# Layer 0 of a streaming encoder step in three parts: the 32-row sample alone first, the second prompt tile's input projection behind the sample's queries

## What is computed

```python
def peer(h, w_query, sub_keys, u_emb, v_emb):
    ...
        qry = (xb @ w_query).astype(f32).reshape(PEER_BLOCK, PEER_HEADS, 2, PEER_DQ // 2)
        sc = jnp.einsum('thpd,pnd->thpn', qry, sub_keys.astype(f32))
        s1, i1 = lax.top_k(sc[:, :, 0], PEER_TOPK)
        s2, i2 = lax.top_k(sc[:, :, 1], PEER_TOPK)
    ...
        top_s, sel = lax.top_k(cand_s, PEER_TOPK)
        idx = jnp.take_along_axis(cand_i, sel, axis=-1)
        gate = jax.nn.softmax(top_s, axis=-1)
        act = jax.nn.gelu(jnp.einsum('thed,td->the', u_emb[idx], xb).astype(f32))
        return jnp.einsum('the,thed->td', (gate * act).astype(xb.dtype), v_emb[idx])

def trunk(x, st_a_conv, st_a_delta, st_b_conv, st_b_h, c_k, c_v, p, past):
    ...
    for l in range(DEPTH):
        h = rmsnorm(x, p['norm_mix'][l])
        ...
        x = x + out
        x = x + peer(rmsnorm(x, p['norm_ffn'][l]), p['peer_w_query'][l], p['peer_sub_keys'][l],
                     p['peer_u'][l], p['peer_v'][l])
```

## Time and profile before

| | us |
|---|---|
| median of 3 runs (lowest, highest) | 1945.54 (1941.55, 1947.11) |
| the profiled execution | 1943.43 |
| its span | 1941.7 |
| PE busy | 1212.1 |
| DVE busy | 1225.5 |
| ACT busy | 723.0 |
| POOL busy | 726.5 |
| TensorE clock granted, mean of the span | 0.738 |

### The profile page before, as it was taken

The page is one execution under the profiler, slowest core; times in us unless marked ns, Lnnn a source line. Parts: engine busy times, 40 slices in busy tenths (PEclk is TensorE's granted clock), DMA queues, the critical chain, the costliest instruction groups (busy, mean ns, idle before and its releaser), DMA issues.

```text
span 1941.7 us, 25073 instructions
## 1 busy us (share of the span) xinstructions
PE 1212.1 (62%) x9288; PEld 739.9 (38%) x9288; DVE 1225.5 (63%) x3079; ACT 723.0 (37%) x1937; POOL 726.5 (37%) x651
## 2 busy tenths in 40 slices
PE   7998865566667539855579546665666644444443
PEld 7896742233335307733248224443325400000000
DVE  4541558888755575476654674557865667677664
ACT  2322145534432335274333333237533334333322
POOL 2021024545433433333133444434533444454442
PEclk9999875676788859966689658778679955555555
DMA  5645389999999999999599999999999999999996
GB/s 192 205 142 162 126 319 397 421 388 421 420 418 418 419 421 393 417 418 393 205 373 416 420 421 417 418 419 414 375 420 418 420 421 422 422 420 422 421 421 273
DMA packets 115658, 720.74 MB, mean 371 GB/s; under 512 B 13424, under 2 KB 13552, under 8 KB 41296
## 3 DMA queue, kind: packets, MB, share of 16 engines
q0 software_dynamic: 82944, 604.02, 75.6%
q1 hardware_dynamic: 31584, 113.84, 15.9%
q10 hardware_dynamic: 1008, 1.29, 0.2%
HBM read 714.98 MB, written 4.12 MB: 370 GB/s over the span
## 4 chain that ended last, share of the span: by engine, by line
DMA 46%; PE 27%; DVE 15%; ACT 6%; issue 4%; POOL 2%; ACTq 0%; POOLq 0%; DVEq 0%; SPq 0%
DMA sb_AR<-in_uv,sb_idx 44%; PE PS L1429 10%; DVE sb_AR L1011 7%; PE PS L1674 5%; PE PS L1651 2%; PE PS L1571 2%; PE PS L1694 1%; POOL sb_AR L513 1%; DMA sb_W<-in_w 1%; ACT sb_DG L576 1%; DVE sb_AR L1063 1%; ACT sb_gl L573 1%; PE PS L1815 1%; ACT L573 1%; DMA sb_lq<-in_lq 1%
## 5 line engine op out<-in xcount | busy, mean ns | idle before, releaser
L513 POOL DMA_INDIRECT sb_AR<-in_uv,sb_idx x576 | 695.2, 1207 | 1042.1 <-PE PS L1674 910.4
L1011 DVE CUSTOM_DVE_ANT_0 sb_AR<-sb_AR 128x1024 f32<-128x1024 f32 x576 | 703.9, 1222 | 452.3 <-DMA sb_AR<-in_uv,sb_idx 447.6
L1674 PE MATMUL PS<-sb_AR,sb_DG 128*32 128x256 f32 x4608 | 509.7, 528 | 582.2 <-ACT sb_DG L576 559.6
L1674 PEld LDWEIGHTS PS<-sb_AR,sb_DG 128*32 128x32 f32 x4608 | 128.9, 129 | 893.7 <-ACT sb_DG L576 802.1
L573 ACT ACTIVATE sb_gl<-sb_dots 128x1 f32<-128x1 f32 x576 | 116.2, 202 | 875.5 <-DVE sb_dots L1011 874.2
L1429 PE MATMUL PS<-sb_hT,sb_W 128*128 128x160 f32 (+1 forms) x2304 | 345.8, 310 | 8.6 <-ACT sb_hT L547 3.3
L1429 PEld LDWEIGHTS PS<-sb_hT,sb_W 128*128 128x128 f32 x2304 | 322.8, 208 | 50.6 <-issue 24.8
L576 ACT ACTIVATE sb_DG<-sb_GR,sb_gl 128x32 f32<-128x32 f32 x576 | 185.1, 321 | 18.7
L573 ACT ACT_TABLE_LOAD x68 | 87.2, 1283 | 1.1
L558 ACT ACTIVATE sb_AR<-sb_Hn 32x1024 f32<-32x1024 f32 x72 | 75.8, 1053 | 1.5
L1651 PE MATMUL PS<-sb_W,sb_mixT 128*128 128x512 f32 x128 | 69.8, 672 | 6.0 <-DMA sb_W<-in_w 4.8
(11 more groups left out here) (357 smaller groups left out, 1193.3 us busy)
## 6 DMA issues: line engine op xcount, KB each, us to landing
sb_W<-in_w SPq DMA_DIRECT2D x192, 512.0 KB, 7.9
sb_AR<-in_uv,sb_idx POOLq DMA_INDIRECT x576, 16.6
sb_gB<-in_gains SPq DMA_DIRECT2D x7, 512.0 KB, 7.7
sb_mixT<-in_kc SPq DMA_DIRECT2D x2, 1024.0 KB, 8.9
sb_hT<-in_vc SPq DMA_DIRECT2D x2, 1024.0 KB, 18.5
out_o_k<-sb_AR SPq DMA_DIRECT2D x1, 1152.0 KB, 9.2
sb_X<-in_x SPq DMA_DIRECT2D x2, 512.0 KB, 7.5
out_o_v<-sb_AR SPq DMA_DIRECT2D x1, 1024.0 KB, 14.3
```

Source lines behind the costliest of these rows:

```text
L513: g.indirect_dma_start(UV[:, sl, :], None, T[f"uv{layer}"], bass.IndirectOffsetOnAxis(ap=idx[:, c:c + 1], axis=0)).then_inc(S(f"uv_in{sl}" ...
L1011: v.tensor_tensor_reduce(UV[:, sl, 0:D], UV[:, sl, 0:D], Hrep[:, u % 2, :], 1.0, 0.0, ALU.mult, ALU.add, dots[:, sl:sl + 1]).then_inc(S("d ...
L1674: r = mm(PS[32 * q:32 * q + 32, 6 + u % 2, 0:256], DG[:, sl, :], UV[:, sl, o:o + 256], start=(c == 0), stop=(c == 31), skip_group_check=True)
```

## The change

Layer 0 is now done in three passes, `TILES = ((2,), (0,), (1,), (2, 0), (1,))`. The first 16 input blocks still run at 160 columns for the sample and tile 0; the other 8 (for `z` and the RG-LRU's gate) stand behind them as `fill` 0 to 7. Then the sample's chunk work goes alone, with 6 stages of inverse instead of 10 (its chunk is 32 long); its output blocks and its queries at 32 columns; `pick(0)`; the first gathers. Tile 0's chunk work stands between the sample's pieces; its output blocks and queries stand beside steps 1 to 24. Tile 1's 24 input blocks are `fill` 8 to 31, behind the sample's queries and beside those steps; its convolutions stand beside steps 21 to 36 and the rest of its mixer beside steps 38 to 141. Output and query weights of layer 0 are loaded once more, so there are 216 block loads.

The order on each engine is now written by `weave`, which merges generators by the keys of `PLAN`. The first 8 gathers use 4 slots only, as the other 4 still hold tile 0's mixer.

```diff
-TILES = ((0, 2), (1,), (2, 0), (1,))
...
+TILES = ((2,), (0,), (1,), (2, 0), (1,))
...
+def slot(m):
+    return m % 4 if m < M4 else (m - M4 + 4) % UVS
+
+
+def slot_before(m):
+
+    return (m - 4 if m >= 4 else None) if m < M4 else (None if m < M4 + 4 else m - UVS)
...
+INV = ["a2", "n2", "n4", "n8", "x1", "m1", "x2", "m2", "x3", "m3"]
+INVS = (INV[0:6], INV, INV)
...
+USES = [((0, "in", j), IN_F[j]) for j in range(16)] + [((2, "fill", n), IN_F[FILL[n][1]]) for n in range(32)]
+for _mp in range(5):
+    if _mp > 2:
+        USES += [((_mp, "qkv", j), B_QKV1 + j) for j in range(24)]
+    USES += [((_mp, "out", j), (B_OUT0, B_OUT1)[_mp > 2] + j) for j in range(8)]
+    USES += [((_mp, "q", j), (B_Q0, B_Q1)[_mp > 2] + j) for j in range(16)]
+USES.sort(key=lambda u: PLAN[u[0]])
+STREAM = [b for _, b in USES]
...
+def weave(*streams):
+
+    heads = [[next(g), k, g] for k, g in enumerate(streams)]
+    while heads:
+        h = min(heads, key=lambda x: x[0:2])
+        t = next(h[2], None)
...
+                    if m == M4:
+                        eng.wait_ge(S("mix_d"), 2)
+                    if b is not None:
+                        eng.wait_ge(S("vsum"), b + 1)
```

```diff
-            caches(0)
-            eng.wait_ge(S("s_qks"), 1)
-            eng.wait_ge(S("pvs"), 1)
-            caches(1)
...
+            eng.wait_ge(S("blk"), POS[2, "out", 7] + 1)
+            cache_k(0)
...
+            cache_v(0)
+            eng.wait_ge(S("s_qks"), 1)
+            cache_k(1)
+            eng.wait_ge(S("pvs"), 1)
+            cache_v(1)
```

More of the change, by code:

```diff
@@ L55, in unit_of @@
     return (2, 0) if k == 0 else ((k - 1) // 4, (k - 1) % 4)
[L58 to L81, removed]
@@ L227, in build @@
         CSi, CSo = a(16, 3), a(16, 6)
+        class VJ:
+            pass
+        class VS:
+            pass
         class V0:
@@ L311, in inv_count, with inv_ps @@
[L311 to L328 removed]
+        def inv_ps(p, name, i):
+            return (i, 0) if p else INV_S[name[0]][i]
@@ L879, in mixer1 @@
                                          ACT.Copy, scale=la_[:, 50:51]).then_inc(S("mix1"), 1)
-                for j in range(8):
-                    upto("out", j)
-                norm(FFN_NORM[mp])
-                upto("norm3")
-                evac_hT(FFN_NORM[mp])
-                queries(mp, upto)
-            mixer1(2)
-            mixer1(3)
-            run.upto(32 * 14 + 8)
-            norm(8)
-            run.upto(NSTEP)
-            norm(9)
+                yield from tail(mp)
+            weave(part0(), gates(0), part1(), fill(), early_hrep(), early_gates(), convs2(), rest(), gates(2), steps())
+            norm(11)
         @block.vector
@@ L907, in rsqrt, with norm @@
                 ch.link(v.tensor_tensor(r, r, w, ALU.mult))
-            def norm(k, last=False, between=lambda: None):
-                tiles = NORMS[k][1]
-                for i, t in enumerate(tiles):
+            def norm(k):
+                for i, t in enumerate(NORMS[k][1]):
                     R = slice(0, ROWS[t])
@@ L1280, in residual, with tail @@
+            def tail(mp):
+                yield at(mp, "norm3")
+                eng.wait_ge(S("blk"), POS[mp, "out", 7] + 1)
                 for t in TILES[mp]:
@@ L1391, in mixer1 @@
                 r.then_inc(S("os_n"), 1)
-                residual(mp, upto)
-                norm(FFN_NORM[mp], between=lambda: upto("norm3"))
-                for j in range(16):
-                    upto("q", j)
-            mixer1(2)
-            mixer1(3)
-            run.upto(32 * 14 + 8)
-            norm(8, last=True)
-            run.upto(NSTEP)
+                yield from tail(mp)
+            weave(part0(), part1(), lru0(), rest(), lru1(), early_picks(), steps())
             peer_add(NUNIT - 1)
-            norm(9, last=True)
+            norm(11)
         @block.tensor
@@ L1828, in mixer1 @@
                     r.then_inc(S("o_tr"), 1)
-                eng.wait_ge(S("mix1"), (4, 6)[ps])
-                out_proj(mp, upto)
-                upto("norm3")
-                transposes(FFN_NORM[mp])
-                hT_ready(FFN_NORM[mp])
-                queries(mp, upto)
-            mixer1(2)
-            mixer1(3)
-            run.upto(NSTEP)
+                yield from tail(mp)
+            weave(part0(), gates(0), part1(), fill(), rest(), steps())
+            assert used[0] == len(STREAM)
 def layout(inputs):
```

1766 lines of the change are left out of this document (913 added, 853 removed), and 6 rows, old and new, of tables (PLAN, _us).

## The result

The changed kernel takes 1975.72 us (median of 4 runs, 1972.66 to 1976.88), the kernel before 1945.18 (4 runs, 1941.55 to 1947.11). The ratio is 1.0161, with a 95% interval of 1.0145 to 1.0177: it is slower by 31 us. The forecast was 1926 with a range up to 1954, so it was wrong in sign and in range. The profiled execution took 1972.66 us, the fastest of the four.

What follows compares the result with a forecast made beforehand. Full DMA engines (419 to 421 GB/s) were taken to bound the long stretches with gathers, so an earlier start should pay. 1943.4 - 16 (gather 32 earlier) + 8 (tile 1's mixer) - 9 (caches) gave 1926 us, range 1891 to 1954.

Steps and rivals of the forecast that it cites:

- Bytes: Whole kernel: 24 more block loads of 0.524 MB, 12.6 MB or 30 us at 421 GB/s.
- cache mechanism: Layer 1: keys of the second half no longer wait for values of the first, removing the wait for caches.
- point of comparison: Gather 32, issued at 341.56 before: all extra blocks used by then, the same work left in both kernels.
- The path to the sample's outputs: Layer 0, ahead of the sample's queries: mixer, inverse, output blocks and norm done by 141 us.
- Nine blocks at 2.1, the first two at up to 3.6: Sample's 32-column query blocks ahead of the first gather: 26 us with tile 0's chunk work between, ending at 167.
- First dot at 192: Behind the first gather, forecast at about 174: five query blocks and the copies, then the first dot product at 192.
- sum 0 at 203: Step 0's sum on PE at 203, behind two input and two output blocks, one waiting for tile 0's mixture.
- 5.1 a step: From sum 0 to sum 24: 5.1 us a step, putting gather 32 at 325, a gain of 16.
- The three limits: Per step from sum 0 to sum 24: PE work 4.7 us, DMA transfers 4.6, landing of blocks 5.1.
- loss 8: Tile 1's convolutions beside steps 21 to 36 load DVE; landed slots absorb 24 us; loss 8, bounds 0 and 20.
- gain 9: Sample's attention in layer 1: no wait for the caches, gain 9 us, bounds 0 and 20.
- Slower: Rival: sums behind slow blocks, 6.2 us or more a step, gather 32 at 352 or later, 1956 us; chance 0.17.

Runs made afterwards that it cites:

- Experiment 2: The changed kernel with 33 useless matmuls filling PE's pauses between the sample's output blocks and its queries, still 32 columns wide; 1973.82 us, ratio 1.0159.
- experiment 1: The changed kernel with the sample's 16 query blocks run over 128 columns instead of 32, the extra results unread; 1956.98 us, ratio 1.0073 to the kernel before.
- Experiments 5: experiment 1 with the four copies of the sample's rows put behind query blocks 2 to 5 on ACT, not behind the last; 1954.27 us, ratio 1.0062.
- experiment 6: Experiments 5's kernel with tile 0's last transposes behind the sample's last query block, and first output and two input blocks behind step 0's sum; 1949.15 us.
- experiment 10: experiment 6 with each of tile 1's convolutions cut to its first of four DVE instructions; 1936.00 us, ratio 0.9964 to the kernel before.
- experiment 3: The changed kernel with layer 1's caches loaded and waited for in the old order; 1995.46 us, ratio 1.0278 to the kernel before.
- experiment 7: The changed kernel with seven of eight matmuls left out of each of tile 1's 24 input blocks, all still loaded; 1984.34 us, ratio 1.0212.
- experiment 8: The changed kernel with only an eighth of the bytes of each of tile 1's 24 input blocks loaded; 1974.12 us, ratio 1.0159.
- experiment 4: The kernel before with the new order of layer 1's caches alone; 1931.75 us, ratio 0.9939 to the kernel before.

## Why the prediction was wrong, step by step

**Bytes, cache mechanism, point of comparison: right.** 733.4 MB moved, and gather 32 was the right place to compare for the transfers: by the windows 645 MB are left there in the kernel before and 646 now. For DVE it is not "the same work": 1049 us of its busy time were left before, 1077 now, as more of tile 1's mixer comes behind it.

**The path to the sample's outputs: right but for 6 us.** The transposes of the normed outputs start at 147.0; the forecast had 141. The ten table loads cost what the row said: from 57.60 to 107, each took 1.28 us, and the activation behind it, where nothing else held it, started at its end:

```profile
57.60 1.28 ACT L749 ACT_TABLE_LOAD   x1
58.89 0.90 ACT L749 ACTIVATE sb_AR<-PS 128x163 f32<-128x163 f32 x4
```

The Trainium skill, "ScalarE: Activation LUTs", section What ACT_TABLE_LOAD costs, adds a drain of 1.38 us to each. The trace does not agree: the activation behind the load starts 0.01 us after its end.

**"Nine blocks at 2.1, the first two at up to 3.6": this is the step that failed first.** From the transposes to `pick(0)` the forecast had 26 us; the trace has 42.3 (147.03 to 189.33). The first two blocks did take 3.4 each, but so did the others, 3.5 to 3.6 (all but the two at 183.53 and 185.66), with half a microsecond of scores that the sum did not have. The price was worked out from 8-column matmuls at a granted 0.95 or so the earlier trace rows, and the pause of PE ahead of the first two (0.43 us in the earlier trace rows) was taken for the reason that they were slow. Experiment 2 shows that it is not the pause; experiment 1 shows that the same blocks, wider, reach 1.00. The rows of before had the warning: a matmul with 8 columns took 0.236 / 2 = 0.118 us a record, one with 128 takes 2.05 / 16 = 0.128 in experiment 1. With 32 columns a block took 1.87 us in the one place where the clock was up and 3.62 where it was down; with 128 columns it took 2.05 up, and 3.74 down (at 220.83). So narrowing a block saved next to nothing at either clock here, and the clock was lost. The first gather came at 198, 24 late: 16 of it is this stretch (13 of them came back in experiment 1), 6 the outputs, and 2 a slip in the forecast's sum, as 167 and 8.8 are 176 and not 174.

The Trainium skill, "TensorE: Matmul & The Clock Gate", Part 1, says that the clock follows how busy PE has been. With busy read as the profile's busy time, this trace does not agree: 48 of 50 us busy at 0.53.

**"First dot at 192", "sum 0 at 203": 29 us behind the first gather were forecast, it took 39.7.** The copies behind the last block, the mixture behind the first dot product (PE waits 5.58 us for it) and the four blocks ahead of the sum were all in the forecast. The half clock was not: the last five query blocks with their scores took 20.9 us (199.97 to 220.90), some twice the forecast's price, and the first dot product came 27 us behind the first gather instead of 18. Without the half clock other waits took much of its place (35.0 us in experiment 1). Experiments 5 and 6 took the queueing away and won 8 us in all; that the rest is PE's work, which has to be done anyway, fits experiment 6 (PE busy for 126 of the 144 us behind its fifth gather) but was not tested.

**"5.1 a step": 5.53.** From the first sum to gather 32 it took 133.5 us, not 122. The three limits were named, but they add up in part: of these 133.5 us PE waits 13.7 for blocks, nearly all of it before 300, and it is full from 300 to 350. The bytes were counted too low as well. The profile's DMA view of the stretch from 238.40 to 371.23:

```profile
DMA packets 10385, 51.14 MB, mean 385 GB/s; under 512 B 1152, under 2 KB 1152, under 8 KB 7083
```

51.1 MB were moved and not 46, 27.0 of them by gathers, where 21 gathers of 1.05 MB had been counted. At 421 GB/s that would be 5.06 us a step; the engines moved 385, although they were busy for 0.99 of the time.

Under all three lies one count that the forecast did not make. PE was busy 269.4 us up to gather 32 before and 305.3 in the changed kernel, and idle 72 and 66. The change gives PE 36 us more to do in a stretch where PE is the busiest engine: 16 query blocks that are run for the sample alone, 14 of them at 3.4 to 3.6 us. In the profile's groups they are 54.5 us of busy time:

```profile
L1550 PE MATMUL PS<-sb_hT,sb_W 128*128 128x32 f32 x256 | 54.5, 387 | 0.0
```

In experiment 1 PE is busy for 287.5 us up to its gather 32, so half of the 36 went with the wide blocks. The kernel before as one window up to gather 32:

```profile
0.00:341.56 341.56, 269.41 (x1984) 223.96 (x1988) 176.27 (x498) 113.41 (x296) 69.01 (x108) 0.87 0.62 221
```

and the changed kernel up to its own:

```profile
0.00:371.23 371.23, 305.27 (x2184) 264.27 (x2184) 150.35 (x414) 117.58 (x301) 62.76 (x106) 0.87 0.65 236
```

**Tile 1's mixer, "loss 8": 16.** "Slots that have landed and wait for DVE take up 16 x 1.5 = 24 us of it, if they are empty before" is the part that fell: DVE is busy 178 of 200 us, and experiment 10 gets 13 us back by shortening the convolutions alone.

**Layer 1's caches, "gain 9": 18 by the windows, 16 by experiment 3, counted from gather 32.** The mechanism was right and the size half.

**The sum mended:** 1926 + 24 (first gather) + 11 (first sum) + 11 (steps) + 8 (mixer) - 9 (caches) = 1971; the profiled execution took 1972.7. Of the rivals "Slower" had the sign, but not the mechanism: it put the loss at 6.2 us a step or more, and the steps took 5.53. A first gather behind 190 was named as the sign that no forecast would hold.

**Open.** The first gather of the kernels with the same front end lies between 198 and 208 in the profiles (the changed kernel, experiments 3, 7 and 8). The traces show where it shifts, and it is the granted clock of the same instructions. Ten input blocks, in the changed kernel and in experiment 8:

```profile
31.89:53.73 21.84, 21.84 (x168) 21.84 (x161) 16.52 (x65) 8.69 (x35) 2.96 (x6) 1.00 0.66 212
33.22:57.36 24.14, 24.14 (x167) 24.14 (x161) 16.62 (x65) 8.68 (x35) 2.96 (x6) 0.90 0.58 193
```

The sample's first query block starts at 150.35 and 156.95, and the rise behind 183.5, which experiments 3 and 8 do not have, makes up the other 3 us. Why one profile has the higher clock stays open. A difference of under 10 us between totals of such kernels need not be the edit's, and is better counted from the point where the edit begins to act. That the division can be made to pay was not shown: in its best form here that computes the same (experiment 6) it is 17 us behind experiment 4, which has the caches alone.

## What to carry to other kernels

Splitting a stage so that a small part goes first makes its matmuls narrow. Price them by rows of the same width and look at the granted clock they run at; if none exists, keep the wide matmul and throw columns away, as in experiment 1. Compare the busy time of the busiest engine up to a point that both kernels pass with the same bytes left, before adding up waits. And where a change has a part that stands by itself, time it alone: here the new cache order was a gain of some 15 us that hid in a loss.

## What the runs showed that was not expected

Query blocks of 32 columns, with their scores between them and PE busy in 20.00 of 20 us, let the granted clock fall from 1.00 to 0.50 (experiment 2), while 128 columns on the same weights raised it from 0.55 to 1.00 (experiment 1). Taking work from PE did not help either: with seven of eight matmuls gone from 24 blocks the clock between 250 and 300 was 0.62 instead of 1.00, and the stretch up to gather 32 took 4 us more (experiment 7). That the clock is the cause of these 4 us was not shown.
